# One-hot rows for the expert gates: both made plain on VectorE, the second scaled by the gates on ScalarE, and late selections compared with a row in PSUM

## The reference, cut to what matters

```python
def peer_ffn(h, wq, keys, u, v):            # per block of 128 tokens
    q = (xb @ wq).reshape(128, 8, 2, 128)
    s = einsum('thpd,hpnd->thpn', q, keys)
    s1, i1 = top_k(s[:, :, 0], 16)          # the two halves of the key
    s2, i2 = top_k(s[:, :, 1], 16)
    cand_s = s1[..., :, None] + s2[..., None, :]        # 16 x 16 candidates
    cand_i = i1[..., :, None] * 128 + i2[..., None, :]  # expert = i1 * 128 + i2
    top_s, pos = top_k(cand_s, 16)
    idx = take_along_axis(cand_i, pos)
    gate = softmax(top_s)
    act = gelu(einsum('thkd,td->thk', u[idx], xb))
    return einsum('thk,thkd->td', gate * act, v[idx])
```

## Time and profile before

| | |
|---|---|
| median of three runs | 3576.49 us (3569.7 to 3577.3) |
| the profiled execution's own time | 3567.22 us |
| its span, first to last instruction | 3565.4 us |
| mean granted TensorE clock | 0.971 |
| TensorE matmul busy | 3325.8 us, 93% |
| VectorE busy | 2685.7 us, 75% |
| ScalarE busy | 1151.8 us, 32% |
| GpSimd busy | 2072.5 us, 58% |
| TensorE L829 (gate products) | 1536 records, 8 for one chunk |
| VectorE L1627, L1632 (one-hots) | 132.4 us and 260.9 us busy |
| VectorE L1578 (pick) | 64 instructions, 106.2 us busy |

### The profile page before, as it was taken

How to read it: one execution, slowest core, us unless ns; L and a number is a source line. 1 busy time by engine, 2 the same in 40 slices (tenths; PEclk the granted TensorE clock), 3 DMA queues, 4 the chain that set the end, 5 groups by cost and what they waited for, 6 DMA issues and landing times. The chain is left out here.

```text
span 3565.4 us, 46813 instructions
## 1 busy us (share of the span) xinstructions
PE 3325.8 (93%) x17370; PEld 2936.9 (82%) x17370; DVE 2685.7 (75%) x5213; ACT 1151.8 (32%) x1914; POOL 2072.5 (58%) x1388
## 2 busy tenths in 40 slices
PE   6997799999989999999989977999999999999996
PEld 5775687999989978888767766889999999788885
DVE  5945349998986578888866633699989765888888
ACT  1234012343434433333212420223443333333332
POOL 5920576776556665555479025767765667555552
PEclk9999899999999999999989988999999999999998
DMA  3210223888778899999723012258887789999994
GB/s 124 86 36 19 77 89 119 277 294 299 278 250 299 307 360 383 354 353 353 259 71 95 13 42 79 75 178 272 295 305 246 274 305 333 359 370 357 354 354 171
DMA packets 312673, 817.10 MB, mean 229 GB/s; under 512 B 22272, under 2 KB 119552, under 8 KB 309120
## 3 DMA queue, kind: packets, MB, share of 16 engines
q1 hardware_dynamic: 112256, 349.02, 28.4%
q0 software_dynamic: 73728, 268.47, 20.2%
q10 hardware_dynamic: 126464, 196.63, 15.8%
HBM read 712.84 MB, written 101.19 MB: 228 GB/s over the span
## 5 line engine op out<-in xcount | busy, mean ns | idle before, releaser
L1192 POOL TENSOR_TENSOR u_lo<-panel,u_hi 128x1024 fp32r<-128x1024 f32 x256 | 615.7, 2406 | 268.2 <-ACT u_hi L1021 266.5
L575 PE MATMUL ps<-hT_hi,u_lo 128*128 128x384 f32 x2048 | 705.9, 345 | 3.9 <-POOL u_lo L1192 3.9
L575 PE MATMUL ps<-hT_hi,u_hi 128*128 128x384 f32 x2048 | 688.4, 336 | 0.0
L575 PE MATMUL ps<-hT_lo,u_hi 128*128 128x384 f32 x2048 | 688.3, 336 | 0.0
L575 PE MATMUL ps<-v_hi,w_lo 128*128 128x512 f32 x1536 | 600.0, 391 | 10.3 <-DVE w_lo L1709 10.2
L575 PE MATMUL ps<-v_lo,w_hi 128*128 128x512 f32 x1536 | 599.4, 390 | 0.0
L575 PE MATMUL ps<-v_hi,w_hi 128*128 128x512 f32 x1536 | 599.2, 390 | 0.0
L1145 POOL TENSOR_TENSOR ring_hi<-panel,cst 128x512 fp32r<-128x512 f32 x244 | 274.6, 1126 | 537.3 <-PE ps L558 303.4
L1207 POOL TENSOR_TENSOR v_lo<-panel,v_hi 128x1024 fp32r<-128x1024 f32 x128 | 315.6, 2466 | 391.3 <-ACT v_hi L1059 391.2
L1021 ACT CAST u_hi<-panel 128x1024 fp32r<-128x1024 f32 x256 | 268.1, 1048 | 708.3 <-PE ps L575 692.0
L1059 ACT CAST v_hi<-panel 128x1024 fp32r<-128x1024 f32 x256 | 269.0, 1052 | 643.3 <-PE ps L575 624.4
(11 more groups left out here) (248 smaller groups left out, 5713.4 us busy)
## 6 DMA issues: line engine op xcount, KB each, us to landing
panel<-in_u SPq DMA_DIRECT2D x256, 512.0 KB, 4.3
panel<-in_v SPq DMA_DIRECT2D x256, 512.0 KB, 7.0
gate_scratch<-arena ACTq DMA_DIRECT2D x24, 2048.0 KB, 9.4
act_scratch<-arena ACTq DMA_DIRECT2D x124, 384.0 KB, 4.3
arena<-act_scratch ACTq DMA_DIRECT2D x62, 768.0 KB, 6.5
arena<-gate_scratch ACTq DMA_DIRECT2D x62, 768.0 KB, 13.7
panel<-in_w_in SPq DMA_DIRECT2D x28, 1024.0 KB, 5.2
panel<-in_wq SPq DMA_DIRECT2D x16, 1024.0 KB, 5.1
```

The lines of the kernel that those rows point to most:

```text
L575: mm = nc.tensor.matmul(o, lhs[a], rhs[b_], start=(start and n == 0), stop=(stop and n == 2))
L1192: pr.mark(nc.gpsimd.tensor_tensor(u_lo[:, j % URING].rearrange("p c n -> p (c n)"), u_tile(j), u_hi[:, j % URING].rearrange("p c n -> p (c ...
```

## The change

It does three things. In `one_hots` both one-hots are plain and made for four tokens by one `tensor_tensor` each, so the four `tensor_scalar` of `hot2` become one instruction. The gates are multiplied in by ScalarE in the new `weigh_hots(k)`, four activations (a copy with a scale from `tabT`) in place on `hot2`; it stands in ScalarE's list right behind `keep_gates(k - 1)`, waits for the new signal `hot_made`, and gives the `hot_ready` that TensorE waits for. And `pick` of token blocks 2 and 3 compares with the row in PSUM in place of the one in SBUF.

```diff
+                def weigh_hots(k):
+                    if k % 32 == 0:
+                        act.wait_ge(tab_ready.sem, layer * tab_ready.per_layer + k // 32 + 1)
+                    act.wait_ge(hot_made.sem, layer * hot_made.per_layer + k + 1)
+                    for c in range(CHUNK):
+                        t = k * CHUNK + c
+                        last = nc.scalar.activation(hot2[:, k % 2, c, :], hot2[:, k % 2, c, :], ACT.Copy,
+                                                    scale=tabT[:, 2, t:t + 1])
+                    pr.mark(last, hot_ready)
...
                     if 0 <= j - FIRST_CHUNK < NG:
                         keep_gates(j - FIRST_CHUNK)
+                    if 0 <= j + 1 - FIRST_CHUNK < NG:
+                        weigh_hots(j + 1 - FIRST_CHUNK)
...
                     if 9 <= k < 17:
                         a = k - 9
+                        places = iota_ps if i > 1 else iota
                         step(nc.vector.tensor_tensor(
-                            pick, iota[:, 0:CAND].rearrange(...).to_broadcast([P, TOPK, CAND]),
+                            pick, places[:, 0:CAND].rearrange(...).to_broadcast([P, TOPK, CAND]),
                             sel_p[:, a, :].rearrange("p (k o) -> p k o", o=1).to_broadcast([P, TOPK, CAND]),
                             ALU.is_equal))
...
-                    firsts = tabT[:, 0:1, k * CHUNK:(k + 1) * CHUNK].rearrange("p o c -> p c o")
-                    nc.vector.tensor_tensor(hot1[:, k % 2], iota_ps.rearrange("p (o n) -> p o n", o=1)
-                                            .to_broadcast([P, CHUNK, NK]), firsts.to_broadcast([P, CHUNK, NK]),
-                                            ALU.is_equal)
-                    for c in range(CHUNK):
-                        t = k * CHUNK + c
-                        last = nc.vector.tensor_scalar(hot2[:, k % 2, c, :], iota_ps, tabT[:, 1, t:t + 1],
-                                                       tabT[:, 2, t:t + 1], ALU.is_equal, ALU.mult)
-                    pr.mark(last, hot_ready)
+                    for n, hot in enumerate((hot1, hot2)):
+                        places = tabT[:, n:n + 1, k * CHUNK:(k + 1) * CHUNK].rearrange("p o c -> p c o")
+                        last = nc.vector.tensor_tensor(hot[:, k % 2], iota_ps.rearrange("p (o n) -> p o n", o=1)
+                                                       .to_broadcast([P, CHUNK, NK]),
+                                                       places.to_broadcast([P, CHUNK, NK]), ALU.is_equal)
+                    pr.mark(last, hot_made)
```

More of the change, by code:

```diff
@@ L365, in build @@
         act_out = [sig(f"act_out{r}", 16 * (UPANELS - 1)) for r in range(2)]
+        hot_made = sig("hot_made", NG)
         hot_ready = sig("hot_ready", NG)
@@ L1577, in routing @@
                         a = k - 9
+                        places = iota_ps if i > 1 else iota
                         step(nc.vector.tensor_tensor(
-                            pick, iota[:, 0:CAND].rearrange("p (o c) -> p o c", o=1).to_broadcast([P, TOPK, CAND]),
+                            pick, places[:, 0:CAND].rearrange("p (o c) -> p o c", o=1).to_broadcast([P, TOPK, CAND]),
                             sel_p[:, a, :].rearrange("p (k o) -> p k o", o=1).to_broadcast([P, TOPK, CAND]),
```

## The result

The changed kernel takes 3530.48 us (median of four runs, 3529.93 to 3543.67), beside 3575.14 for the kernel before (four runs, 3569.7 to 3577.3): a ratio of 0.9881 with an interval of 0.9855 to 0.9906. That is 45 us by the medians and 42 by the ratio.

What follows compares the result with a forecast made beforehand. TensorE was taken as the bound, 5.06 us a chunk, except in late stretches and at the start, where it waits for VectorE. 19.8 - 1.4 + 2.0 = 20.4 us off 3567.2 gives 3546.8, plus 9.3 is 3556; 8 in 10 from 3538 to 3571.

Steps and rivals of the forecast that it cites:

- the start of `u_lo`: Block 3 heads' turns: GpSimd's `u_lo` runs 1.33 to 3.70 us behind D(k), so the multiply waits and ends at 4.56.
- the late stretch: Turns 46 to 59, where block 3 is routed: G(50) to G(61) takes some 67 us in both layers.
- Rival 1: Block 3 heads: the multiply isn't caught, a head's turn is 5.42 us, -42 us, 3534; chance 8 in 100.
- The cast of turn 49: L1573 on VectorE: still waits for `u_lo` and ends where it ends now, 1.94 us long; turn 49 saves nothing.
- The cast of turn 58: L1588 on VectorE: still waits for `u_lo` and ends where it ends now, 1.90 us long; turn 58 saves nothing.
- Rival 2: Turns 49 and 58: the casts win their race with `u_lo`; -26 us in all, 3550; chance 12 in 100.
- the recorded shift of 1.85 us by D(50): Second layer, turns 46 to 49: turn 46 gives 0.5 us, 47 and 48 give 0.68 each, 49 nothing.
- The comparison in PSUM: L1578 in block 3 on VectorE: takes 0.99 us, bounds 0.98 to 1.08, and doesn't wait for GpSimd.
- The ScalarE group: Four activations for each chunk on ScalarE take 1.26 us, bounds 1.2 to 1.55.
- The 6.77 us of a locked turn: A head's turn in turns 50 to 57, multiply caught by `u_lo`: 7.79 - 1.02 = 6.77 us.
- Tile 32: Tile with two table loads on ScalarE: no cover for the activations, 0.7 us lost in each layer.
- The start of the stage: G(1)'s wait: L1548 may escape `u_lo`; 2.0 us gained together, bounds a 0.65 loss in each layer to 4.6 gained.

Runs made afterwards that it cites:

- the kernel that was kept late: Changed kernel with three more 800-element PSUM comparisons on VectorE in turn 49, ahead of the cast, both layers: 3557.22 us, ratio 0.9960 to the kernel before.
- 500 more elements: Changed kernel with one more 500-element PSUM comparison on VectorE ahead of the head in each of turns 50 to 57: 3551.31 us, ratio 0.9944 to the kernel before.
- one more comparison: Changed kernel with one more 800-element PSUM comparison on VectorE in turn 49, once in each layer: 3534.35 us, ratio 0.9883 to the kernel before.
- the kernel with the one-hots alone: Changed kernel with the comparison back on the SBUF row, keeping the one-hots and ScalarE's scaling: 3537.98 us, ratio 0.9906 to the kernel before.
- the odd turns: Changed kernel with block 2's routing steps in turns 1, 3, ... 27, not 0, 2, ... 26: 3527.03 us, then 3524.19; ratio 0.9866 to the kernel before both times.

## Why the prediction was wrong

**The step that failed** is the start of `u_lo`: "L1582 would start at 2.23, in the middle of `u_lo` (1.33 to 3.70)". That GpSimd is 1.33 us behind D(k) was read from a turn in which VectorE was late, and taken over into a kernel in which it would be less so. The wait in that row, 4.44 us for a `dot`, says that the phase (where `u_lo` stands in VectorE's turn) is VectorE's own doing. What the runs showed in its place: `u_lo` 4.94 to 2.77 us behind D(k), the multiply 0.99 us and not 2.3, a head's turn 5.41 us and not 6.77, the late stretch 56.3 and not 67.

The question was when VectorE stops being late. In the kernel before it is in time in turn 46 and late from turn 48 on, as GpSimd's rows of that trace show:

```profile
2693.04 2.39 POOL L1192 TENSOR_TENSOR u_lo<-panel,u_hi 128x1024 fp32r<-128x1024 f32 x1 [1.56 <-ACT u_hi L1021]
...
2707.24 0.95 POOL L1174 DMA_INDIRECT arena<-in_u_rows,arena  x1 [1.70 <-DVE arena L1641]
2708.21 2.41 POOL L1192 TENSOR_TENSOR u_lo<-panel,u_hi 128x1024 fp32r<-128x1024 f32 x1
```

Two sums would have told. The first, an estimate from that trace: left to ScalarE, `u_lo` starts 0.24 us behind D(46) and then every 5.05, so 20.44 and 25.49 behind it. D(50) was 24.91 behind D(46); take off 4 x 0.68 for the one-hots and 1.72 for a free cast (1.94 less the 0.22 that it takes undisturbed in block 2), and it is 20.47, a distance of 5.0. The cast would start at 18.9, when the `u_lo` before it (15.39 to 17.8) is over, so it is indeed free. The second: a free turn less TensorE's 5.05 us, times eight, says whether that distance lasts. Rival 1 had the free turn, 5.42, measured 5.41, and its price, 3534 beside 3530 measured. But it was put as a property of the instruction ("the multiply isn't caught"), and given 8 in 100 since the other rows show that such instructions do wait. They do: 1671, 2340 and up to 3200 ns in the experiments. It didn't wait for `u_lo` here, since it began first.

**The cast of turn 49** was the first piece of it. It was to stay at 1.94 us and lasted 0.22, by the same mistake: the shorter turns 46 to 48 put VectorE in time, and `u_lo` (954.97) began 1.48 us behind the cast. The cast of turn 58 lasted 0.22 too. Rival 2 had the free cast, but gave turns 50 to 57 the locked phase all the same. By the estimate above this piece mattered: with the cast caught, the recorded shift of 1.85 us by D(50) leaves a distance of 2.4, enough for one head.

**The size of the miss** is 25.5 us. The gate stages have 19.2 of it (39.6 us less, 20.4 forecast). The other 6 lie between one profiled execution and the medians, for which the forecast had added 9.3; the runs don't say what makes them.

**Right in size.** The comparison in PSUM, 0.98 us and free of GpSimd (0.99 said). Both one-hots at 685 ns a piece. The ScalarE group, 1.28 us (1.26 said). The 6.77 us of a locked turn, 6.76 in the kernel that was kept late. A cast that is caught, 1.9 to 2.6 us said, 2.58 and 2.59 in turn 58 where VectorE was late again (500 more elements, one more comparison).

The Trainium skill's rule ("SBUF — State Buffer", section "Who interferes with whom") holds in what it says of operands: one in PSUM, never over 982 ns in the changed kernel; two in SBUF, up to 3.38 us beside `u_lo` in the kernel with the one-hots alone. That whoever starts first keeps the port is borne out for the multiply from both sides, by the 2.70 us of `u_lo` in turn 57 and by the `u_lo` that came 0.12 us ahead. But the starts that the profile lists don't settle a close race: the comparison listed 0.12 us ahead of `u_lo` lost it, as did L1548 with 0.41. The rule says who waits once they meet, not whether they meet.

**The small terms.** Tile 32 loses 0.47 us a layer and the next 0.1 (0.7 said); around tile 76, where ScalarE loads tables too, two chunks take 5.27 and 5.16, 0.3 in all, which the sum hadn't. The start of the stage was to gain 2.0 and gains nothing: from G(0) to G(2) the two layers took 11.10 and 14.21 us before, and 11.26 and 14.40 after. L1548 did escape, as hoped, but the additions behind it on VectorE now run beside two `u_lo` and take 7.61 us where they took 4.74, and G(1) comes no earlier. VectorE's turn 0 in the first layer, then G(1) in the second on TensorE, after the change:

```profile
703.09 0.22 DVE L1562 TENSOR_SCALAR arena<-arena 128x128 f32<-128x128 f32 x1
703.34 7.61 DVE L1567 TENSOR_TENSOR work<-arena 128x128 f32<-128x128 f32 x16
```

```profile
2462.61 2.08 PE L830 MATMUL ps<-arena 128*128 128x128 f32 x8 [2.47 <-ACT arena L1059]
```

The start has two lengths. In two of three profiles of the changed kernel the first layer's takes 14.4 us from G(0) to G(2), in one 11.26. Half of the difference is only where G(0) stands. In the short start TensorE ran tile 24, ahead of G(0), at a mean granted clock of 0.71, so for a part of it at the lower of its two levels (1.2 and 2.4 GHz), and took 5.8 us where the second layer took 4.3 at 1.00. G(0) is then 7.08 us behind D(0) and not 5.51, while G(1) is 13.2 behind it in both. In the long start the clock is 1.00 up to G(1) and 0.75 in the tile behind it: after a wait of 2.47 us, G(1) to G(2) takes 6.71 us, and 5.18 in the short start, where the wait was 0.86 and the clock 1.00. So from D(0) to G(2) the two differ by 1.6 us. With the odd turns G(0) stands at 5.5, G(2) comes 11.1 us later in all four stages, and the granted clock is 1.00 from tile 24 to G(2).

In block 2's turns, where TensorE is the bound, the multiply does meet `u_lo` (1.27 us in the median, 2.04 at most, where it took 0.99), and that costs nothing.

**Left open:** why the clock falls in tile 24 in some stages, behind G(1) in others, and in two (first layer with one more comparison, second layer with the one-hots alone) in neither, though TensorE waited for `u_lo` ahead of tile 24 equally long in both starts of the first profile (2.25 and 2.24 us); and what makes the 1.3 us by which the odd turns gain more in the medians than in the stages (both kernels' runs spread over 6 to 7 us).

## What to carry to other kernels

The phase between two engines is a result of the schedule, not a constant of it: before pricing a collision, ask who releases each party in the new schedule, and read in the trace whether the wait ahead of it names the engine whose lateness you are removing. Where one engine's lateness makes the collision that keeps it late, count the distance at the start of the stretch and the slip of each turn (turn less the pace of the bounding engine). The turns before the distance runs out are free, those behind it are locked, and a few microseconds of work in the wrong turn lock them all: three took back 12 of the 20 us in each layer.

## What the runs showed that was not expected

One microsecond of VectorE work ahead of a stretch cost 2 us in each layer, three of them 12. A VectorE instruction with both operands in SBUF that meets GpSimd's `u_lo` waits for all that is left of it and then takes its own time, to within 0.15 us: 3.12 us for 0.99, when `u_lo` had begun 0.12 us before. The reverse holds as well, with 2.70 us for a `u_lo` of 2.40.
